# Mixed attention in fp32 on one Trainium2 core: index scores ahead of a unit's division, and the search rounds of the sparse heads dealt out anew

## The reference

```python
h = _rmsnorm(x, mix_norm[l])
(qa, ka, va, qb, kb, vb, qc, ckv, qidx, kidx, widx) = _split_cols(h @ w_in[l])
out_a = _sliding_window_attn(qa, ka, va, attn_sinks[l], tab_a)   # 8 heads, window 128, with sinks
out_b = _moba_attn(qb, kb, vb, tab_b)                            # 4 heads, here plain causal
kv_c = _rmsnorm(ckv, kv_norm_c[l]) @ w_kv_up_c[l]
out_c = _dsa_attn(qc, kv_c[..., :64], kv_c[..., 64:], qidx, kidx, widx * 0.5, tab_c)   # 4 sparse heads
x = x + jnp.concatenate([out_a, out_b, out_c], axis=-1) @ w_out[l]
```

```python
dots = jnp.einsum('bqhd,bsd->bqhs', qi, k_idx) * (IDX_DIM ** -0.5)
score = jnp.einsum('bqhs,bqh->bqs', jax.nn.relu(dots), wi)
score = jnp.where(key_pos[None, :] <= tq[:, None], score, -jnp.inf)
_, idx = lax.top_k(score, n_keep)                                # n_keep = 128
```

## Time and profile before

| | us |
|---|---|
| median of 3 runs | 3269.54 (3268.1 to 3269.61) |
| the profiled execution, its time | 3267.59 |
| its span | 3265.8 |
| PE busy in the span | 3176.6 |
| DVE, ACT, POOL busy | 1768.4, 1158.3, 536.2 |
| first mix stage, from about | 391.6 to 624 |
| second mix stage, from about | 1343.9 to 1576 |

### The profile page before, as it was taken

The page is one execution under the profiler, slowest core; times in us unless marked ns, Lnnn a source line. Parts: engine busy times, 40 slices in busy tenths (PEclk is TensorE's granted clock), DMA queues, the critical chain, the costliest instruction groups (busy, mean ns, idle before and its releaser), DMA issues.

```text
span 3265.8 us, 42562 instructions
## 1 busy us (share of the span) xinstructions
PE 3176.6 (97%) x14834; PEld 2552.1 (78%) x14834; DVE 1768.4 (54%) x2767; ACT 1158.3 (35%) x1878; POOL 536.2 (16%) x482
## 2 busy tenths in 40 slices
PE   8999999999999999998999999999999999999998
PEld 6888876788888888776888878667888886778887
DVE  4434477543445344585543454557647556576474
ACT  4323245322223222354322232634324325344242
POOL 0000345200020001254100030231000422310003
PEclk9999999999999999999999999999999999999999
DMA  4354331233333333221333323112333231223332
GB/s 124 98 141 141 107 89 33 84 101 92 96 97 97 103 90 102 78 62 38 93 104 89 106 74 116 39 58 72 105 88 105 62 99 46 59 66 102 93 98 79
DMA packets 540649, 287.98 MB, mean 88 GB/s; under 512 B 13603, under 2 KB 536582, under 8 KB 540544
## 3 DMA queue, kind: packets, MB, share of 16 engines
q1 hardware_dynamic: 535936, 273.32, 29.0%
q0 software_dynamic: 4608, 13.30, 1.4%
HBM read 284.30 MB, written 10.02 MB: 90 GB/s over the span
## 4 chain that ended last, share of the span: by engine, by line
PE 84%; DVE 9%; issue 3%; ACT 2%; POOL 1%; DVEq 0%; DMA 0%; ACTq 0%; POOLq 0%
PE bank L1816 68%; PE bank L1830 4%; PE bank L2054 2%; PE bank L1847 2%; PE bank L2096 2%; PE bank L1910 2%; PE bank L2119 1%; DVE w_lo L1232 1%; ACT w_hi L786 1%; DVE norm_t L1317 1%; POOL probs L680 1%; DVE score L1476 1%; ACT tap_v L925 0%; PE bank L1868 0%; DVE top L1475 0%
## 5 line engine op out<-in xcount | busy, mean ns | idle before, releaser
L786 ACT ACTIVATE w_hi<-w_raw 128x1024 fp32r<-128x1024 f32 (+2 forms) x477 | 533.2, 1119 | 1426.0 <-PE bank L1816 788.2
L1816 PE MATMUL bank<-h_hi,w_hi 128*128 128x512 f32 x2548 | 1001.0, 393 | 7.1 <-DVE h_lo L1257 3.7
L1816 PE MATMUL bank<-h_hi,w_lo 128*128 128x512 f32 x2548 | 992.8, 390 | 0.0
L1816 PE MATMUL bank<-h_lo,w_hi 128*128 128x512 f32 x2536 | 987.8, 390 | 0.0
L1232 DVE TENSOR_TENSOR w_lo<-w_raw,w_hi 128x1024 fp32r<-128x1024 f32 (+1 forms) x445 | 619.5, 1393 | 467.7 <-ACT w_hi L786 467.6
L1816 PEld LDWEIGHTS bank<-h_hi,w_hi 128*128 128x128 f32 x2548 | 477.9, 188 | 119.3 <-issue 14.5
L1816 PEld LDWEIGHTS bank<-h_hi,w_lo 128*128 128x128 f32 x2548 | 477.9, 188 | 101.1
L1816 PEld LDWEIGHTS bank<-h_lo,w_hi 128*128 128x128 f32 x2536 | 476.0, 188 | 99.7 <-issue 1.9
L1816 PE MATMUL bank<-act_hi,w_hi 128*128 128x512 f32 x924 | 360.4, 390 | 0.0
L1816 PE MATMUL bank<-act_lo,w_hi 128*128 128x512 f32 x924 | 360.1, 390 | 0.0
L1816 PE MATMUL bank<-act_hi,w_lo 128*128 128x512 f32 x924 | 360.1, 390 | 0.0
(11 more groups left out here) (323 smaller groups left out, 4010.3 us busy)
## 6 DMA issues: line engine op xcount, KB each, us to landing
w_raw<-in_ffn_w_gate_dram SPq DMA_DIRECT2D x88, 512.0 KB, 3.8
w_raw<-in_ffn_w_up_dram SPq DMA_DIRECT2D x88, 512.0 KB, 3.8
w_raw<-in_ffn_w_down_dram SPq DMA_DIRECT2D x64, 704.0 KB, 4.5
w_raw<-in_ffn_w_in_dram SPq DMA_DIRECT2D x88, 512.0 KB, 3.8
w_raw<-in_ffn_w_out_dram SPq DMA_DIRECT2D x32, 704.0 KB, 4.5
w_raw<-in_w_in_dram SPq DMA_DIRECT2D x34, 512.0 KB, 3.7
w_raw<-in_a_w_qkv_dram SPq DMA_DIRECT2D x24, 512.0 KB, 3.8
w_raw<-in_w_out_dram SPq DMA_DIRECT2D x16, 512.0 KB, 3.6
```

The lines of the kernel that those rows point to most:

```text
L786: nc.scalar.activation(w_hi[c % 2][:, 0:nk, 0:cols], raw[c % 2][:, 0:nk, 0:cols], ACT.Copy).then_inc(hi_ready, 1)
L1816: mm = nc.tensor.matmul(result(c)[0:cols, :], w[b][:, k, 0:cols], x[k], start=(k == 0 and n == 0), stop=(k == nk - 1 and n == 2))
```

## The change

Five edits, in the two mix stages:

1. In the loop over the units, DVE takes the index scores at i = 4, 5, 6 before it divides unit c+i and makes `w_lo`, where it took them behind.
2. `ROUNDS` brings tile 3's 16 rounds to an end at i = 10 (before: 15 of them by i = 11), so that no round stands between the last division and the first pair's maxima.
3. `SLOT_ROUNDS` deals out the rest anew: cumulated counts in slots -1 to 5.
4. `pair_max` writes the sink columns of a head once a pair, four columns in one copy, where it wrote one ahead of each of the pieces: 2 copies for 8.
5. On POOL, in the first mix stage, two DMAs of bias rows are issued behind the masking of the score tile instead of ahead of it.

```diff
-        ROUNDS = {5: 1, 6: 3, 7: 3, 8: 6, 9: 9, 10: 12, 11: 15}
-        SLOT_ROUNDS = [18, 22, 26, 30, 34, 41, 48]
+        ROUNDS = {4: 1, 5: 2, 6: 5, 7: 6, 8: 10, 9: 13, 10: 16}
+        SLOT_ROUNDS = [19, 23, 27, 32, 38, 44, 48]
...
                     for j, t in enumerate(T_ORDER):
-                        if MIX[name] == 0 and j < 2:
-                            spread_bias(bias_far, 1, T, slice(2 * j + 4, 2 * j + 6), c + 7 + j)
                         if j == 2:
                             low(BASE[name] + POOL_LOW[0])
                         pool.wait_ge(score_ready, 3 * MIX[name] + j + 1)
...
+                        if MIX[name] == 0 and j < 2:
+                            spread_bias(bias_far, 1, T, slice(2 * j + 4, 2 * j + 6), c + 7 + j)
...
+                for x in range(2 if plan["narrow"] and ph == 0 else 0):
+                    n = 2 * p + x
+                    if p and x == 0:
+                        dve.wait_ge(p_ready, NT * (JOB[stage] + 2 * p))
+                    nc.vector.tensor_copy(BIASED2[kind(stage)][x][:, P:P + 3 * (NEAR + 1) + 1:NEAR + 1],
+                                          nsinks[:, MIX[stage], n:n + 1].broadcast_to([P, NT]))
...
-                    if plan["narrow"]:
-                        nc.vector.tensor_copy(BIASED2[kind(stage)][x][:, to + w:to + w + 1], floor)
...
-                        divided(c + i, proj[cols, cb, :], 0, cols)
-                        if i >= 2 and c + i + 2 < c + POOL_LOW[0]:
-                            lo(c + i + 2)
                         if i == 4:
...
                         if i in (4, 5, 6):
                             index_scores(name, i - 4)
+                        divided(c + i, proj[cols, cb, :], 0, cols)
+                        if i >= 2 and c + i + 2 < c + POOL_LOW[0]:
+                            lo(c + i + 2)
```

## The result

| | us |
|---|---|
| before, median of 5 runs | 3268.1 (3266.1 to 3269.6) |
| changed, median of 5 runs | 3252.0 (3242.0 to 3253.5) |
| ratio, 95% interval | 0.9945 (0.9932 to 0.9958) |
| the profiled execution of the changed kernel | 3242.04, span 3240.3 |

The changed kernel is faster, by 0.55%. The ratio puts it at 0.9945 x 3268.1 = 3250.1 us, a gain of 18.0 us against the 14.0 forecast and just past the low end of the predicted range, 3251. Timed again beside the first three experiments it took 3252.7 against 3266.7, ratio 0.996 (0.9946 to 0.9973), a gain of 13 us.

What follows compares the result with a forecast made beforehand. PE, busy 97%, was taken to bound the kernel. Terms of 3.7 + 1.7 + 1.6 = 7.0 us a stage, 14.0 for two, took 3269.5 to 3255.5 us; 8-in-10 range 3251 to 3260.5.

Steps and rivals of the forecast that it cites:

- Term 1: First pair's maxima: PE's wait for them goes, the chain over ACT and POOL moves; 3.7 us a stage, bounds 2.0 to 3.7.
- the rival of a hidden tail: ACT can't take the first exponential right behind its table load; 2.6 us for both stages, chance 0.08.
- PE's new wait: Before turning pair 0, near 472, PE waits 2.2 us for POOL's scaling, where it was not held before.
- Term 2: Tile 2's penalty leaves slot 3, so POOL scales pair 4 sooner; 1.7 us a stage, bounds 0.9 to 1.8.
- Term 3: Tile 1's penalty in slot 5 comes sooner with four rounds for seven; 1.6 us a stage, bounds 1.5 and 2.2.
- The clock behind the new wait: Rival: the clock falls behind PE's wait for POOL at pair 0 in both stages, 1.7 us each; 3259, chance 0.3.
- The failed step: Slot 5: a shorter penalty wait may bring a shorter slow stretch, up to 1.4 us more, not counted in the forecast.
- What costs nothing: Index scores ahead of the division, moved rounds, sink copies and bias DMAs in the mix stages, all costed at nothing.
- A gift: Rival in slot 5: shorter slow stretch (1.4 us) and DVE's scaling not held (0.6), 2.0 a stage; 3251.5, chance 0.15.
- Nearly everything there comes from three places: PE's first-stage waits: 5.2 us for a penalty, 4.5 for pair maxima, 1.3 for POOL's scaling.
- The "packed" first part: Rival: 16 rounds between i = 4 and i = 10 make DVE late with a division; slower, chance 0.02.
- six rounds late: Size given for DVE's late divisions in the stage's first part: 9.1 us, the kernel then taking 3273.7.

Runs made afterwards that it cites:

- the first three experiments: Changed kernel with slots' table of before, 0.9965; kernel before with only the slots' table changed, 0.9989; changed kernel with both tables of before, 0.9996.

## Where the prediction was right, and the step that failed

The three terms were priced rightly. The forecast came out too small because it put two things at nothing, the clock behind the penalty's wait and the first part of the stage.

**Term 1** was 3.7; piece C measures 3.68 less. The chain over ACT and POOL sets the end, as the working had it. In the changed kernel ACT's timeline reads:

```profile
458.72 1.28 ACT L988 ACT_TABLE_LOAD   x1
460.02 0.51 ACT L988 ACTIVATE probs<-biased,nmax 128x257 f32<-128x257 f32 x1
```

The first exponential stands right behind the load, and the rival of a hidden tail falls. By an estimate from the 2.66 us of the Trainium skill (ScalarE: Activation LUTs, What ACT_TABLE_LOAD costs) it would have begun at 461.4; the measurement decides for 1.28. PE's new wait wasn't 2.2 us in one piece. The first step of turning needs only the first two scalings, so it came as 0.42 and 1.25. It ended where the working put it: 471.84 there, less the 2.20 by which this execution's stage begins earlier and the 0.48 of A and B, is 469.16, and the row has 469.27.

**Term 2** was 1.7; D measures 1.6. POOL's scaling of pair 4 now starts right behind its `w_lo`, in POOL's timeline:

```profile
505.93 2.40 POOL L687 TENSOR_TENSOR w_lo<-w_raw,w_hi 128x1024 fp32r<-128x1024 f32 x1 [1.60 <-ACT w_hi L786]
508.31 8.51 POOL L680 TENSOR_SCALAR probs<-probs,recip 128x512 f32<-128x512 f32 x8
```

A wait of PE for POOL of 0.74 is left at 515.07. The penalty at its new place took 0.51 us and not 2.45, though POOL's scalings of pair 3 were running (497.73 to 504.33):

```profile
501.51 0.51 DVE L1478 TENSOR_SCALAR pen<-score 128x384 fp32r<-128x384 f32 x1
```

It took 0.36 there in the run with two rounds fewer in slot 5. So at the new place it was not held to the end of a scaling, as the prediction had thought possible, and PE did not wait for it.

**Term 3** was 1.6; E measures 1.7, and that is partly luck. The working had 1.2 us ahead of the second part's maxima and took off 0.6 for DVE's own scaling. The maxima begin at 532.76. That is 541.69 less the 7.94 us by which the changed kernel is ahead of before at the end of D, and less another 1.0. The scaling was held for only 0.3, 1.20 us for two where it had been 0.88:

```profile
534.34 1.20 DVE L1543 TENSOR_SCALAR probs<-probs,recip 128x512 f32<-128x512 f32 x2
```

With the 0.98 of the round behind the division it makes 1.7. The two errors nearly cancel. The new table also takes one round out of slot 4 (six for seven), which the prediction doesn't price; the waits of PE show no place for it.

**The clock behind the new wait**, rival at 0.3, was priced rightly (1.6 us for 1.7, where two stages of one program differ by it alone) but comes and goes. Of the 14 stages profiled with this wait unfilled it fell in 7. In the forecast's own profile it fell in neither, in the second one in one.

**The failed step** is this one: "That would be up to 1.4 us more; I don't count it". Piece F won 1.3 us in all four profiled stages of the changed kernel, 2.6 for two. With the 7.0 of the terms (6.9 measured) it makes 8.2 of the 8.7 us that a stage is shorter. The other term at nothing is "What costs nothing": A and B won 0.5 us a stage, all of it from the edits outside the tables (no run takes these three apart). Counting both takes the gain from 14.0 to 17.4 us; from the 3268.1 measured beside it that is 3250.7, and the ratio has 3250.1. (1.4 us of the way from 3255.5 to there is the kernel before, which was at 3269.5 for the forecast.) It is the larger part of the rival "A gift", to which I gave 0.15.

I had no ground to count on it, though, and its reason there, a shorter wait with a shorter slow stretch behind it, isn't borne out. In four profiled stages with a 3.5 us wait in other kernels F was 7.7, 7.5, 6.3 and 4.8; in four with the old 5.17 us wait and edits that don't touch it F was 6.9, 7.0, 6.3 and 7.7; and after 2.47 us it was 7.7 and 7.8. What is shown is that F's excess over 4.8 is clock, since filling the wait removes it. That the change is what lowered it from 7.6 to 6.3 isn't shown; the 7.6 is from one profile of the kernel before. What sets the length of the slow stretch stays open.

Two smaller slips stand in the prediction. "Nearly everything there comes from three places" passes over 2.6 us for DVE's `w_lo` and 0.9 us for its `h_lo` in the same list of waits, which the change doesn't touch. And the chances of a gain over 0.2% add up to 0.94, not 0.93.

**Not seen at all** was what the edit to the order is for. I costed the index scores ahead of the division at nothing, and alone they and the small edits win 0.5 us a stage. But without that order the changed kernel loses 8.5 us in one stage and 3.7 in the other. A and B have 7.0 and 5.4 of it, more than the first table wins in C; the rest, up in one stage and down in the other, is the clock that comes and goes in D and F. The "packed" first part was a rival with the right mechanism (DVE late) and the wrong victim: not a division but the normed keys at i = 7. My "six rounds late" wasn't needed for it: one round more, and one more step held up by POOL's `w_lo`, are enough. The rule of the Trainium skill (SBUF — State Buffer, Who interferes with whom), that whichever of DVE and POOL holds the shared port pair blocks the other to the end of its instruction, agrees with the 2.82 us for 0.75.

## What to carry to other kernels

Price a wait of a busy PE twice: its idle time, and the clock behind it, which here came as 0 to 3.0 us behind waits of 1.25 to 5.2 us. Don't count on a shorter wait to lower the second price; filling the wait did. When a table packs an engine more tightly, look at each of its results that another engine waits for, not only at the one next to the edit; an edit that wins next to nothing alone may be what makes the table possible. And hold single executions against each other by the pieces between equal instructions, not by their totals.

## What the runs showed of the hardware

- The granted clock after the same wait isn't settled by the program or by the length of the wait. After 1.25 us idle at the turning of pair 0 it was 1.00 in one execution and 0.58 in another. After 3.5 us for the penalty F took 4.8 to 7.7 us, after 2.47 us 7.7, and after 5.2 us 6.3 to 7.7. After 3.7 us for the normed keys B took 21.5 in one stage and 20.0 in the other, against 18.5.
- Matmuls that compute nothing, put into the wait, kept the clock at 1.00 behind it in all 8 stages in which they were tried, and F was 4.82 to 4.83 in each. Of 14 stages with the wait unfilled one came to 4.84.
- In code that the change doesn't touch, two executions of one program took 2912.5 and 2921.5 us. It isn't idle time: PE was idle for 61.5 and 58.1 us of it. The mean granted clocks of the two executions were 0.995 and 0.990.
- DVE's `scalar_tensor_tensor` of 512 columns took 2.82 us beside POOL's `w_lo`, 0.75 without it; three of 256 columns took 3.54 for 1.52.
